# Second layer's branch inputs and the triangle inversion: low halves moved to VectorE, taps in pieces, transposes in place of a second product

## What is computed

```python
def _conv_branch(p, dw_w, dw_b, ln_g, ln_b):
    z = p[..., :CV_W] * jax.nn.sigmoid(p[..., CV_W:])
    z = _dwconv(z, dw_w, dw_b)
    return jax.nn.silu(_layernorm(z, ln_g, ln_b))
```

```python
    L = jnp.where(strict, jnp.einsum('bhnid,bhnjd->bhnij', kb, k) * decay, 0.0)
    T = lax.linalg.triangular_solve(eye + L, jnp.broadcast_to(eye, L.shape),
                                    left_side=True, lower=True, unit_diagonal=True)
    u = jnp.einsum('bhnij,bhnjd->bhnid', T, v * beta[..., None])
    w = jnp.einsum('bhnij,bhnjd->bhnid', T, kb * jnp.exp(gc)[..., None])
    a_intra = jnp.where(incl, jnp.einsum('bhnid,bhnjd->bhnij', q, k) * decay, 0.0)
```

## Time and profile before

| | us |
|---|---|
| median of 3 runs | 4384.47 |
| lowest and highest run | 4380.95, 4391.7 |
| the profiled execution, its own time | 4386.48 |
| its span in the profile | 4384.7 |

### The profile page before, as it was taken

One profiled execution on the slowest core, in us unless ns is written; L12 is line 12 of the kernel. 1 busy time (PEld: TensorE's weight loads), 2 busy tenths in 40 slices (PEclk: granted clock), 3 DMA queues, 4 the chain that ended last, 5 costly groups with the idle time before them and its releaser, 6 DMA issues. The chain is left out here.

```text
span 4384.7 us, 62679 instructions
## 1 busy us (share of the span) xinstructions
PE 4096.1 (93%) x25302; PEld 3582.4 (82%) x25302; DVE 2724.1 (62%) x5388; ACT 1825.0 (42%) x2340; POOL 461.9 (11%) x130
## 2 busy tenths in 40 slices
PE   7999899999999999999889899999998988888798
PEld 5876788788877888888778789998887977878697
DVE  5735678899931555555585687745665745643674
ACT  3433333477733222222245445444444423543453
POOL 2222034100000000000134230000000030000000
PEclk9999999999999999999899999999998988998999
DMA  7422224477787777777434456678885401645264
GB/s 247 140 90 72 91 89 145 150 290 270 293 326 279 239 241 243 243 243 243 155 120 148 150 182 229 239 285 278 290 288 201 153 1 58 188 142 164 68 189 139
DMA packets 523626, 833.18 MB, mean 190 GB/s; under 512 B 20813, under 2 KB 398861, under 8 KB 502057
## 3 DMA queue, kind: packets, MB, share of 16 engines
q1 hardware_dynamic: 523338, 829.18, 56.5%
HBM read 692.19 MB, written 136.92 MB: 189 GB/s over the span
## 5 line engine op out<-in xcount | busy, mean ns | idle before, releaser
L113 PE MATMUL bank<-hThi_l,pr_whi 128*128 128x512 f32 (+1 forms) x2304 | 786.1, 341 | 19.4 <-POOL pr_wlo L1907 12.7
L113 PE MATMUL bank<-hTlo_l,pr_whi 128*128 128x512 f32 (+1 forms) x2304 | 778.6, 338 | 0.0
L113 PE MATMUL bank<-hThi_l,pr_wlo 128*128 128x512 f32 (+1 forms) x2304 | 777.7, 338 | 0.0
L113 PE MATMUL bank<-pr_whi,pr_ahi 128*128 128x512 f32 x1536 | 599.5, 390 | 6.5 <-DVE pr_alo L2274 6.4
L113 PE MATMUL bank<-pr_whi,pr_alo 128*128 128x512 f32 x1536 | 598.9, 390 | 0.0
L113 PE MATMUL bank<-pr_wlo,pr_ahi 128*128 128x512 f32 x1536 | 598.9, 390 | 0.0
L2032 ACT ACTIVATE pr_whi<-pr_w 128x2048 fp32r<-128x2048 f32 x270 | 517.7, 1917 | 126.8 <-DMA pr_w<-peer_v_in 124.3
L113 PEld LDWEIGHTS bank<-hThi_l,pr_whi 128*128 128x128 f32 x2304 | 441.0, 191 | 68.7 <-POOL pr_wlo L1907 14.5
L113 PEld LDWEIGHTS bank<-hThi_l,pr_wlo 128*128 128x128 f32 x2304 | 440.3, 191 | 45.9
L113 PEld LDWEIGHTS bank<-hTlo_l,pr_whi 128*128 128x128 f32 x2304 | 441.0, 191 | 42.0
L2150 DVE TENSOR_TENSOR pr_wlo<-pr_w,pr_whi 128x2048 fp32r<-128x2048 f32 x102 | 236.0, 2314 | 272.6 <-ACT pr_whi L2032 272.5
(11 more groups left out here) (608 smaller groups left out, 8692.4 us busy)
## 6 DMA issues: line engine op xcount, KB each, us to landing
pr_w<-peer_u_in SPq DMA_DIRECT2D x128, 1024.0 KB, 5.7
pr_w<-peer_v_in SPq DMA_DIRECT2D x128, 1024.0 KB, 5.0
dense_weights<-pr_buf SPq DMA_DIRECT2D x20, 4096.0 KB, 16.5
pr_g<-dense_weights SPq DMA_DIRECT2D x64, 1024.0 KB, 9.1
gu_w<-ffn_w_up_in SPq DMA_DIRECT2D x88, 512.0 KB, 4.8
gr_w<-w_in_in SPq DMA_DIRECT2D x32, 1024.0 KB, 5.3
expert_scores<-pr_s SPq DMA_DIRECT2D x64, 512.0 KB, 7.2
pr_gs<-expert_scores SPq DMA_DIRECT2D x64, 512.0 KB, 5.9
```

The lines of the kernel that those rows point to most:

```text
L113: ins = pe.matmul(psum, a, b, start=first and i == 0, stop=last and i == len(terms) - 1)
```

## The change

In `project`, a list `amid` may give VectorE a piece of work for each part, run after the next part's low half and after the parts before it are evacuated. In the second layer's `branch_inputs`, the low halves move from GpSimd to VectorE, `cv_conv` no longer follows its part, and the taps of the two channel tiles alternate, each waiting for the same tile's tap before it, in pieces of taps 0 to 4, 5 to 9, 10 to 18, 19 to 22, 23 to 26 and 27 to 30. The next stage's low half comes last. The first layer's call is unchanged.

In `solve_triangles`, the sums of all groups get banks of their own (0 to 3) and run ahead of the products; the products use bank pairs (4, 5), (6, 7), (0, 1), (2, 3). VectorE folds beta into its product with the key products (`times_keys`), so GpSimd only masks, for levels 0 and 1 at once. The first inverse is `ident - mid` on VectorE, transposed by TensorE and copied by ScalarE. In levels 1 to 5 the second joining product and its subtraction are replaced by a transpose of the new `inv_t` on TensorE and a copy on ScalarE (`turn_inverse`, `take_inverse`); level 6 starts with the last of these transposes.

```diff
...
             for n in range(len(parts)):
                 if lo_on == "vector" and n + 1 < len(parts):
                     split_lo(dve, n + 1)
+                if amid and amid[n:]:
+                    dve.wait_ge(free, of_part[n][0])
+                    amid[n](dve, chain)
                 for i in of_part[n] if follows[n] else []:
-                    if then and not side and i == last_follow:
+                    if then and not side and not amid and i == last_follow:
                         then.split_lo(dve, then_hi)
                     dve.wait_ge(free, i + 1)
                     last = follows[n][0](dve, chain, parts[n][5] + items[i][1])
                     if follows[n][1]:
                         last.then_inc(followed, 1)
-            if then and side:
+            if then and (side or amid):
                 then.split_lo(dve, then_hi)
...
                     chain(ins)
             return ins
 
+        def taps_of_both(first, end):
+            def run(dve, chain):
+                dsts = [by_stream(y[:, j, t0:TALL], ns) for j in range(2)]
+                if first == 0:
+                    for j in range(2):
+                        mid = a[:, j, s0:2, PAD:PAD + CTX]
+                        last = dve.tensor_tensor(mid, mid, b[:, j, s0:2, :], ALU.mult)
+                    chain(last)
+                for tap in range(first, end):
+                    for j, dst in enumerate(dsts):
+                        src, scalar = a[:, j, s0:2, tap:tap + CTX], w[:, j, tap:tap + 1]
+                        if tap == 0:
+                            ins = dve.tensor_scalar(dst, src, scalar, wb[:, j:j + 1], ALU.mult, ALU.add)
+                        else:
+                            dve.wait_ge(chain.sem, tap_of[(tap - 1, j)])
+                            ins = dve.scalar_tensor_tensor(out=dst, in0=src, scalar=scalar, in1=dst, op0=ALU.mult, op1=ALU.add)
+                        chain.count += 1
+                        ins.then_inc(chain.sem, 1)
+                        tap_of[(tap, j)] = chain.count
+            return run
+
+        tap_of = {}
+        nothing = lambda dve, chain: None
+        amid = None if side else [nothing, nothing] + [taps_of_both(*ends) for ends in ((0, 5), (5, 10), (10, 19), (19, 23), (23, 27), (27, CV_K))]
+
...
-            (CV_OFF, 2 * MIX, True, (t0, TALL), cv_in, (cv_conv, None)),
+            (CV_OFF, 2 * MIX, True, (t0, TALL), cv_in, None if amid else (cv_conv, None)),
...
+            (O_OFF, MIX, False, tiles, copy_to(lambda o, t: osig[:, t, :], ACT.Sigmoid))], width=MIX + 16, ring=2, buffers=ring, ahead=2, side=side, late_finish=True, then=then, before_follow=padding, lo_on="vector" if amid else "gpsimd", amid=amid,
...
+        def pair_bank(n):
+            return (4, 6, 0, 2)[n]
...
             @block.gpsimd
             def _(pool):
                 for n in range(4):
-                    t, hg = divmod(n, 2)
-                    pool.wait_ge(read, n + 1)
-                    pool.tensor_tensor(low[:, n, :, :], low[:, n, :, :], over_heads(beta[:, t, :], hg), ALU.mult).then_inc(lowed, 1)
                     pool.wait_ge(lowed, n + 1)
-                    pool.tensor_tensor(part[:, n, :, :], low[:, n, :, :], level[:, 0, :][:, None, :].broadcast_to([P, 4, P]), ALU.mult).then_inc(parted, 1)
+                    pool.tensor_tensor(mid[:, n, :, :], low[:, n, :, :], level[:, 0, :][:, None, :].broadcast_to([P, 4, P]), ALU.mult).then_inc(paired, 1)
+                    pool.tensor_tensor(part[:, n, :, :], low[:, n, :, :], level[:, 1, :][:, None, :].broadcast_to([P, 4, P]), ALU.mult).then_inc(parted, 1)
...
-                    for n in range(4):
+                    for n in range(4 if lv > 1 else 0):
                         m = 4 * (lv - 1) + n
-                        if lv == 1:
-                            pool.wait_ge(based, n + 1)
-                        else:
-                            pool.wait_ge(mid_psum, m - 3)
+                        pool.wait_ge(mid_psum, m - 3)
...
+                def sums(n):
+                    t, hg = divmod(n, 2)
+                    for i in range(4):
+                        h = 4 * hg + i
+                        last = pe.matmul(K.ps[n][:, i * P:(i + 1) * P], g[:, t, h:h + 1].broadcast_to([P, P]), K.tri[:, :], start=True, stop=True)
+                    last.then_inc(rowed, 1)
+
...
-                        pe.wait_ge(read, n - 1)
-                    b = 3 * (n % 2)
+                        pe.wait_ge(ranged, 2 * (n - 1))
+                    b = pair_bank(n)
...
+
+                sums(0)
+                sums(1)
+                key_products(0)
+                sums(2)
+                key_products(1)
+                sums(3)
+                key_products(2)
+                key_products(3)
                 for n in range(4):
-                    pe.wait_ge(parted, n + 1)
-                    if n >= 2:
-                        pe.wait_ge(based, n - 1)
+                    pe.wait_ge(inverted, n + 1)
+                    pe.wait_ge(read, n // 2 + 1)
                     for i in range(4):
-                        last = pe.transpose(K.ps[6 + n % 2][:, i * P:(i + 1) * P], part[:, n, i, :], K.ident[:, :])
+                        last = pe.transpose(K.ps[4 + n][:, i * P:(i + 1) * P], inv[:, n, i, :], K.ident[:, :])
...
+                def join(lv, n):
+                    m = 4 * (lv - 1) + n
+                    pe.wait_ge(mid_copied, m + 1)
+                    if m >= 4:
+                        pe.wait_ge(inv_copied, m - 3)
+                    if m >= 2:
+                        pe.wait_ge(subbed, m - 1)
+                    elif m == 1:
+                        pe.wait_ge(based, 4)
...
+                def turn_inverse(lv, n):
+                    m = 4 * (lv - 1) + n
+                    pe.wait_ge(subbed, m + 1)
+                    if m >= 2:
+                        pe.wait_ge(inv_copied, m - 1)
+                    b = 5 + 2 * (n % 2)
+                    for i in range(4):
+                        last = pe.transpose(K.ps[b][:, i * P:(i + 1) * P], inv_t[:, n, i, :], K.ident[:, :])
...
-                        for i in range(4):
-                            if lv < LAST:
-                                pe.matmul(K.ps[b][:, i * P:(i + 1) * P], inv[:, n, i, :], mid[:, n, i, :], start=True, stop=True)
-                                last = pe.matmul(K.ps[b + 1][:, i * P:(i + 1) * P], mid[:, n, i, :], inv[:, n, i, :], start=True, stop=True)
-                            else:
...
+                    middle(lv, 0)
+                    if lv > 1:
+                        turn_inverse(lv - 1, 3)
+                    for n in range(1, 4):
+                        middle(lv, n)
+                    join(lv, 0)
+                    for n in range(1, 4):
+                        join(lv, n)
+                        if lv < LAST:
+                            turn_inverse(lv, n - 1)
...
+                def take_inverse(m):
+                    act.wait_ge(inv_turned, m + 1)
+                    act.activation(inv[:, m % 4, :, :], heads_of(5 + 2 * (m % 2)), ACT.Copy).then_inc(inv_copied, 1)
...
+                def times_keys(n):
+                    t, hg = divmod(n, 2)
                     dve.wait_ge(exped, n + 1)
-                    dve.tensor_tensor(low[:, n, :, :], low[:, n, :, :], heads_of(b + 1), ALU.mult)
-                    dve.scalar_tensor_tensor(out=att[:, n, :, :], in0=heads_of(b + 2), scalar=SCALE, in1=att[:, n, :, :],
+                    dve.wait_ge(pe_done, n + 1)
+                    for i in range(4):
+                        h = 4 * hg + i
+                        last = dve.scalar_tensor_tensor(out=low[:, n, i, :], in0=low[:, n, i, :], scalar=beta[:, t, h:h + 1],
+                                                        in1=K.ps[pair_bank(n)][:, i * P:(i + 1) * P], op0=ALU.mult, op1=ALU.mult)
+                    last.then_inc(lowed, 1)
+
+                def times_queries(n):
+                    dve.scalar_tensor_tensor(out=att[:, n, :, :], in0=heads_of(pair_bank(n) + 1), scalar=SCALE, in1=att[:, n, :, :],
                                              op0=ALU.mult, op1=ALU.mult).then_inc(read, 1)
 
+                def first_inverse(n):
+                    dve.wait_ge(paired, n + 1)
+                    dve.tensor_tensor(inv[:, n, :, :], K.ident[:, None, :].broadcast_to([P, 4, P]), mid[:, n, :, :], ALU.subtract).then_inc(inverted, 1)
+
                 range_of(0)
-                for n in range(4):
-                    if n < 3:
-                        range_of(n + 1)
-                    times_products(n)
-                ident = K.ident[:, None, :].broadcast_to([P, 4, P])
-                for n in range(4):
-                    dve.wait_ge(parted, n + 1)
-                    dve.tensor_tensor(inv[:, n, :, :], ident, part[:, n, :, :], ALU.subtract)
-                    dve.wait_ge(turned, n + 1)
```

(14 more changed lines are left out.)

## The result

The changed kernel took 4360.58 us (median of 4 runs, 4357.98 to 4362.58), the kernel before 4385.68 in the same comparison (4380.95 to 4391.7): a ratio of 0.9942, interval 0.9924 to 0.9959, that is 25 us less, 18 to 33. The profiled execution took 4360.11, its span is 4358.3.

A forecast was written before the change was run, and what follows sets the result against it. TensorE, busy 93% of the span, was taken to bound the kernel, with holes at both changed places. Branch inputs -8.8 and triangle stage -20.4 (-12.3 - 8.7 + 0.6) gave -29.2 from 4384.5: 4355.3 us, own range 4347 to 4367, 8-in-10 range 4346 to 4368.

The forecast's parts named there:

- TensorE's waits for low halves: Branch inputs: TensorE's 4.4 us of waits for GpSimd's low halves go once VectorE makes them.
- Taps at 0.40 us: Branch inputs: alternating taps overlap on VectorE, 0.40 us each, 3.2 us for a piece of 8; without overlap 0.485 each.
- The end of the stage: Branch inputs: Silu starts 1.7 us after the last evacuation, four take 2.3, ending at 2244.6 against 2253.35.
- Branch inputs: Second layer's branch inputs as a whole: 8.8 us shorter, bounds 6.5 to 10.
- Prologue: Triangle stage before its levels: VectorE's chain sets it, 22.4 us instead of 34.7, so -12.3; bounds 21.5 to 25.
- Levels: Triangle levels 1 to 5: 9.0 us a level plus 1.6 for level 1's slow start, 46.6 against 55.3, -8.7.
- Level 6: Triangle stage's last level: four transposes and a copy on its path, +0.6 us, for 4.6 before.
- The sum: Whole kernel: branch inputs -8.8 and triangle stage -20.4 give -29.2 us, from 4384.5 to 4355.3.
- Rival 1: Prologue and taps give part back: lower clock +3.5, lock +1.5, no tap overlap +1.5; 4361.8 us, chance 0.12.
- Rival 2: Transposes keep the levels at 1.2 GHz: 17.9 us a level instead of 9.0; 4399.8 us, chance 0.04.
- Rival 3: Branch inputs' end is not the limit, so only the triangle stage gains: 4364.1 us, chance 0.04.
- a later stage longer than before: Sign that the prediction is wrong: a stage behind the branch inputs or triangle stage takes longer than before; no size given.

The follow-up runs named there:

- a_only: Only the new branch inputs, with the old `solve_triangles`, against the kernel before: 4380.20 us (11 runs), ratio 0.9980 (0.9971 to 0.9989).
- prologue_only: New triangle prologue, but both joining products and subtractions in levels 1 to 5 and the branch inputs as before, against the kernel before: 4378.29 us, ratio 0.9977.
- b_only: Only the new `solve_triangles`, with the old branch inputs, against the kernel before: 4369.58 us (5 runs), ratio 0.9958 (0.9945 to 0.9972).
- mids_first: Changed kernel with GpSimd's level 0 masks of groups 2 and 3 ahead of their level 1 masks: 4357.28 us, ratio 0.9927 to the kernel before.
- taps_serial: a_only with each tap waiting for the instruction just before it, so none overlap: 4383.53 us in one execution (kernel before 4389.81).
- pieces_serial_lo_gpsimd: New branch inputs alone, but low halves on GpSimd and taps never overlapping, against the kernel before: 4387.26 us, ratio 0.9993 (0.9984 to 1.0003).
- after_again: The changed kernel once more, unedited, against the kernel before: 4359.84 us (5 runs), ratio 0.9938 (0.9925 to 0.9952).

## Why the prediction was right, step by step

The forecast was 4355.3 us with a range of 4346 to 4368; the time is 4360.6, inside the range and inside the forecast's own 4347 to 4367. Its mechanism held at each step. Some sizes inside the steps were off, and partly cancelled.

- **TensorE's waits for low halves** go: right, none is left. The last evacuation came 2240.66 - 2169.82 = 70.84 us after the stage's start instead of 2244.99 - 2169.05 = 75.94, 5.1 less where the step had 4.4; it had said that each wait might cost somewhat more than its recorded idle time.
- **Taps at 0.40 us**: right (0.40 apart, 3.25 for 8 against 3.2), none longer than 0.48. The low half waited 0.22 for ScalarE at 2231.52, so VectorE was ready in time.
- **The end of the stage**, 1.7 to the Silu and 2.3 for four: 1.70 and 2.19. Branch inputs -8.8 forecast; -9.6 in the trace and -9.8 at an equal clock; -8.8 in `a_only`'s ratio.
- **Prologue** -12.3 (22.4 us): 21.97, 21.98 and 21.95 in the three traces of this order with the new levels, 21.05 in `prologue_only`, which began at the full clock. The fourth group's key products were to start after 12.4 us; TensorE got its bank after 3555.70 - 3543.14 = 12.56. They ran at the full clock (2.06 us, where 3.5 was assumed), so VectorE was done with them after 16.4 us and not 17. The lock between VectorE and GpSimd was put at 1.8 us for the four first inverses: 0.68, 1.35, 1.16 and 1.16 against 0.68 undisturbed are 1.6. The last four transposes took 0.9 where 0.5 was assumed, since they ran at half clock. The Trainium skill, page "SBUF — State Buffer", section "SBUF: two separate sides", states this lock: of a VectorE instruction with two SBUF inputs and a GpSimd instruction that reads SBUF, the one that starts first has the shared port pair for the whole instruction, and the other one blocks. The rows agree: where a VectorE inverse had begun first (3557.20), GpSimd's mask took 1.65 us instead of 1.27.
- **Levels** at 9.0: right, 9.00, 9.01, 9.00 and 9.09 for levels 2 to 5. Level 1 was given 10.6 and took 9.64 here and 11.01 in `b_only`. Two things lie behind that. The sum gave level 1 sixteen transposes, but it holds twelve: the last four of each level stand in the next one, and those of level 5 were counted again in level 6, 0.45 us too much. And its slow start lasts as long as the lower clock lasts into it, granted 0.88 on average here and 0.77 in `b_only`. Its windows in the two:

```profile
3565.11:3574.75 9.64, 9.64 (x78) 9.56 (x77) 2.30 (x4) 4.18 (x7) 7.60 (x6) 0.88 0.00 0
```

```profile
3577.37:3588.38 11.01, 11.01 (x78) 10.93 (x77) 2.30 (x4) 4.18 (x7) 7.70 (x6) 0.77 0.01 1
```

Levels 1 to 5 -8.7 forecast, -9.5 and -8.2 measured.

- **Level 6** +0.6: +0.62.
- **The sum** -29.2. The traces give -31.2 at these places; the ratios of the two comparisons give -25 and -27, with intervals that reach -33. What separates them is no step of the sum but the spread of the rest, above all of the expert stage. The spread of 4 us that the range allowed for is too small for single executions (12 us in that stage alone), enough for these medians.

**Rival 1** (prologue and taps give part back) did not come: the granted clock rose within the prologue, 0.81 on average, the lock cost 1.6 us and not 3.3, and the taps overlapped. Its 4361.8 is nearer to the measured 4360.6 than the forecast's 4355.3, so the time alone would speak for it; the rows decide against it.

**Rival 2** (the transposes bring the clock down) fell: levels 2 to 5 have 16 transposes each and ran at clock 1.00 in 9.00 us; at the lower level it would have been 17.9. They ran at 2.4 GHz throughout. The rule of the Trainium skill that the prediction cited (page "TensorE: Matmul & The Clock Gate", section "Part 4: PE-mode transpose"), that the full clock doesn't engage for transposes, isn't what these rows show where matmuls stand around them. In the prologue, the first four transposes, after a pause of 0.18 us, ran at 2.4 GHz as well (0.66 us); the other three groups, after pauses of 2.24, 0.57 and 0.57 us, ran at 1.2 GHz (1.11 to 1.12 us for four). In `mids_first` the second group too took 0.66 us, after a pause of 1.58. Whether the pauses or the transposes themselves lowered the clock no run here tells apart.

**Rival 3** (the branch inputs' end is not the limit) fell: the next stage's first instruction moved with it, and `a_only`, where its condition gives nothing, is faster by 0.2%.

The prediction said that a later stage longer than before would speak against it. One was, by 5.7 us, and only the repetition and the halves alone showed that it meant nothing. One trace of each kernel is not enough to say where 5 of 4360 us went.

## What to carry to other kernels

When an engine with slack takes over work that another engine waits for, the size of the pieces it does in between decides: 8 taps (3.25 us) between two low halves cost TensorE nothing, 60 and two q/k followers cost it 14.0 us. Where a pair of results costs two fp32 products of two passes each and one result is the transpose of the other, a transpose of one pass and a copy on an idle engine is cheaper (9.00 us a level instead of 10.72) if something else lies between the result and its transpose. And look at stretched instructions first: the long taps of the kernel before were VectorE waiting for a GpSimd instruction to end, and moving GpSimd's work to VectorE, with the pieces, brought 9.0 us of that stage at an equal clock even with taps that don't overlap, the overlap 0.9 more.

## What was not expected of the hardware

**Overlapping VectorE instructions shut GpSimd out.** A row of 34 alternating taps with two SBUF inputs each, 0.40 us apart, kept a GpSimd subtraction waiting for 7.3 us (11.9 instead of 4.6); with each tap waiting for the one before, the same subtraction took 4.75. The page "SBUF — State Buffer" of the Trainium skill, named above, has the winner hold the ports for one instruction. Here each tap began before the last one had ended (0.40 apart, 0.48 long), and GpSimd came no further until the whole row was done. The trace of the kernel before could not show that, since there every tap waited for its forerunner.

**The clock at a stage's start moves the stage.** The old prologue, not one instruction changed, took 34.83 us in `a_only` and 32.17 in `taps_serial`. The first sums on TensorE's timeline and the window of the prologue, of `a_only` and then of `taps_serial`:

```profile
3536.64 0.76 PE L2633 MATMUL bank<-tri,gd_g 128*128 128x128 f32 x2 [0.98 <-PEq L61]
```

```profile
3536.60:3571.40 34.80, 20.37 (x112) 19.01 (x112) 19.44 (x47) 4.60 (x8) 11.61 (x10) 0.70 0.00 0
```

```profile
3543.28 0.46 PE L2633 MATMUL bank<-tri,gd_g 128*128 128x128 f32 x2 [0.98 <-PEq L61]
```

```profile
3543.20:3575.40 32.20, 17.65 (x112) 16.29 (x112) 19.45 (x47) 4.60 (x8) 11.63 (x10) 0.81 0.00 0
```

The granted clock is 0.70 in the one and 0.81 in the other; TensorE's busy time is 2.7 us less, and so is the prologue. It is the start that counts. Six traces have the old prologue: the two whose first 8 us ran at 1.00 (`taps_serial` and `pieces_serial_lo_gpsimd`) took 32.17 us, the four at 0.77 to 0.80 took 34.5 to 34.8. With the new prologue, the clock's mean over all of it was 0.81 in the changed kernel and 0.89 in `after_again`, and both took 22.0, since both began at the lower one. Part of it comes back: level 1 took 13.22 us in `taps_serial` and 12.27 in `a_only`, so that the triangle stages differ by 1.7 us and not by 2.7. `chain_of_states` has two durations as well: 24.9 us in the six executions whose clock went down in its first 4 us (0.57 to 0.59 on average in them; the kernel before, `a_only` and `b_only` are three), 23.3 in the six where it stayed at 1.00 there (`taps_serial` and the changed kernel are two), with the old triangle code as with the new. So of the 1.6 us that the profiled execution gained there, nothing is put down to the change.
